# Turning the second 128 prompt queries' probabilities on VectorE instead of TensorE

## The chip, the cores and the metric

One Trainium2 chip, one NeuronCore. The metric is the device time of one execution in microseconds; lower is better. The time before is the median of three runs, 1886.21 us (1886.2 to 1886.69).

## The reference: one layer of a hybrid streaming encoder

There are 320 tokens: 64 of a sample (with 128 cached positions) and 256 of a prompt. All of them go through one layer:

```
u = rmsnorm(h) @ w_in            # q, k, v of mixer A (chunk band) and of mixer B (forgetting), forget logits, two gates
scores = q @ k^T * scale + bias  # 8 heads x 128 in each mixer; bias is a table (A) or F[t] - F[s] (B), masked
probs  = softmax(scores)
o      = probs @ v
h += (sigmoid(gate_A) * (o_A @ w_a) + sigmoid(gate_B) * (o_B @ w_b)) @ w_o
h += relu(rmsnorm(h) @ w_up)^2 @ w_down
h += (p @ w_ple_proj) * sigmoid(rmsnorm(h) @ w_ple_gate)
y  = rmsnorm(h)
```

In the attention of one head and mixer the prompt has two groups of 128 queries. The first group sees 128 keys, so its probabilities are a 128x128 block. The second group sees 256 keys, so it has two such blocks. The sample's 64 queries see 192 keys.

## The kernel before

**Layout.** Activations are kept transposed: 128 features in the partitions, 320 tokens in the columns. Every weight matrix is cut into slabs of 128 output columns and 1024 input rows. Two slabs make a panel, which is one 128x320 product. A slab is loaded by SP (512 KB, four slots), rounded by ScalarE to its high part (`split_weights`, L628), and VectorE takes the low part as the rest (`split_weights`, L945). TensorE multiplies a slab in 24 matmuls (L395 to L397: high by high, high by low, low by high). TensorE waits for a slab at `s_wlo`, which VectorE counts up after L945. ScalarE waits at `s_mul` until TensorE is through with the slab that last filled the slot, and SP waits at `s_wlo` until the raw slab in it was read.

**Units.** There are 16 attention units: 8 heads by 2 mixers, written (head, mixer). While TensorE multiplies the three panels (q, k, v) of one unit, the attention of the unit before runs in the gaps. TensorE's order in `unit` (L446) is: panel t; `attend` of the unit two back; `scores` of the unit before; panel t+1; the first half of panel t+2; `turn` of the unit before; the second half of panel t+2. Unit (0,0) to (1,0) are handled by straight-line code, then a loop over the heads 2 to 7 holds two units in its body. The last units end beside the first panels of the merge stage (L510 to L512): after the first half of the first merge panel come `attend` of (7,0) and `scores` of (7,1), in the middle of the second merge panel comes `turn` of (7,1), and after that panel `attend` of (7,1).

**The path of the probabilities.** VectorE adds the bias and finds the maxima (`logits`, L984 to L990), ScalarE takes the exponentials (L688), VectorE the reciprocal of their sums (`invert`, L996), and GpSimd multiplies by it (`normalise`, L1346), in the order first prompt group, second prompt group, sample, each counting `s_prob` up. To multiply with the values, the probabilities must stand with the keys in the partitions. For the prompt, TensorE turns three 128x128 blocks against an identity (`turn`, L424 to L426) into the bank TURNED, and ScalarE copies 384 columns to `probs_t` (`copy_turned`, L695). For the sample, VectorE turns them in squares of 32x32, two squares in an instruction, eight instructions (`turn_sample`, L1028). VectorE turns the values in the same manner, 16 instructions of three squares (`turn_values`, L1017). `attend` (L428) waits for the copy, for the sample's turn (`s_sturned`) and for the values.

**VectorE's order.** It is written out by hand in its own `unit` (L1138): take q out of its bank; low part of slab (t+2, half 0); `split_output`, the low part of the attention output (L1002); `logits`; slab (t+2, half 1); `invert`; `turn_values`; take k out; slab (t+3, half 0); `turn_sample`; slab (t+3, half 1); take v out; both slabs of panel t+4. Unit (0,0) has its own straight line (L1130 to L1136): take k out, split panel 6, take v out, `turn_values`, `turn_sample`, split panel 7. The last unit too has its own (L1185 to L1200).

Of the kernel before, what the change touches and what calls it, by code (L numbers as in the profile page):

```python
# [21 lines left out]
ACT = mybir.ActivationFunctionType  # L22
AX_X = mybir.AxisListType.X

P = 128
# [24 lines left out]
P0, P1, P2 = S1, S1 + P, S1 + P + SEQ  # L50
# [4 lines left out]
T_MERGE = T_UNIT + 3 * UNITS  # L55
# [65 lines left out]
def hybrid_layer(nc, io):  # L121
    from contextlib import ExitStack

    with ExitStack() as ctx:
        def sb(name, shape, dt=F32):
            return ctx.enter_context(nc.sbuf_tensor(name, shape, dt))

        def sem(name):
            return ctx.enter_context(nc.semaphore(name))
# [26 lines left out]
        ident = sb("ident", [P, P])  # L156
# [21 lines left out]
        probs = sb("probs", [P, P2])  # L178
        probs_t = sb("probs_t", [P, 512])
# [3 lines left out]
        banks = ctx.enter_context(nc.psum_tensor("banks", [P, 8, 512], F32))  # L183
        SCORES, SAMPLE, VALUES, TURNED = 4, 5, 6, 7
# [21 lines left out]
        def f32(ap):  # L206
            return ap.bitcast(F32)
# [62 lines left out]
        s_prob = sem("probs_ready")  # L270
        s_vrows = sem("value_rows_ready")
        s_sturned = sem("sample_probs_turned")
        s_turn = sem("prompt_probs_turned")
        s_tcopy = sem("turned_prompt_probs_ready")
        s_pv = sem("attended")
# [34 lines left out]
        def after(eng, s, value):  # L310
            if not isinstance(value, int) or value > 0:
                eng.wait_ge(s, value)
# [55 lines left out]
        def _(pe):  # L368
            def multiply(t, hi, lo, ready=None, value=None, bank_read=False, second=None, between=None, base=0):

                pe_bank = base + t.half
                if bank_read:

                    pe.wait_ge(s_acc, t.first - 1)
                for half in range(2):
                    if half and between:  # L380
                        between()

                    pe.wait_ge(s_wlo, t.count(2, half + 1))
                    slot = 2 * t.half + half
                    for kk in range(SLAB_KB):
                        k = half * SLAB_KB + kk
                        if k == KB - 1 and ready:

                            pe.wait_ge(ready, value)
                        bank = pe_bank if second is None or half == 0 else second  # L390
                        out = banks[:, bank, 0:TOK]
                        ws = slice(kk * P, (kk + 1) * P)
                        xs = slice(k * TOK, (k + 1) * TOK)
                        lo_k, hi_k = (0, KB - 1) if second is None else (half * SLAB_KB, half * SLAB_KB + SLAB_KB - 1)
                        nc.tensor.matmul(out, w_hi[:, slot, ws], hi[:, xs], start=k == lo_k, stop=False)  # L395
                        nc.tensor.matmul(out, w_hi[:, slot, ws], lo[:, xs], start=False, stop=False)  # L396
                        mm = nc.tensor.matmul(out, w_lo[:, slot, ws], hi[:, xs], start=False, stop=k == hi_k)  # L397
                    mm.then_inc(s_mul, 1)
# [16 lines left out]
                nc.tensor.matmul(banks[:, SCORES, P:P + SEQ], q[:, NEW + P:TOK], k[:, S1:KEYS], start=True, stop=True)  # L415
                nc.tensor.matmul(banks[:, SAMPLE, S0:S1], q[:, 0:P], k[:, 0:S1], start=True, stop=True).then_inc(s_score, 1)  # L416

            def turn(u):

                pe.wait_ge(s_prob, u.count(3, 2))  # L420

                after(pe, s_tcopy, u.count())
                b = banks[:, TURNED, 0:3 * P]
                nc.tensor.transpose(b[:, 0:P], probs[:, P0:P1], ident[:, :])  # L424
                nc.tensor.transpose(b[:, P:2 * P], probs[:, P1:P1 + P], ident[:, :])
                nc.tensor.transpose(b[:, 2 * P:3 * P], probs[:, P1 + P:P2], ident[:, :]).then_inc(s_turn, 1)  # L426

            def attend(u):  # L428

# [13 lines left out]
            def mix_in(t, between=None, bank_read=False):  # L443
                multiply(t, x_hi, x_lo, between=between, bank_read=bank_read)
# [55 lines left out]
            with pe.Fori(2, HEADS) as i:  # L500
                t = Panel(T_UNIT, 6, i)
                unit(t, Unit(i - 1, 0), Unit(i - 1, 1))
                unit(t.plus(3), Unit(i - 1, 1), Unit(i, 0))
            last = Unit(HEADS - 1, 1)
# [3 lines left out]
                scores(last)  # L508

            mix_in(Panel(T_MERGE), between=last_scores)  # L510
            mix_in(Panel(T_MERGE + 1), between=lambda: turn(last))
            attend(last)  # L512
            merge(Panel(T_MERGE + 2), first=True)
            mix_in(Panel(T_MERGE + 3))
# [2 lines left out]
            with pe.Fori(1, KB // 2) as i:  # L517
                t = Panel(T_MERGE, 6, i)
# [34 lines left out]
            for s in range(4):  # L553
# [6 lines left out]
                for n in range(4):  # L560
                    out = banks[:, 4 * (1 - s % 2) + n, 0:TOK]
                    for k in range(2):
                        b = 2 * n + k
# [57 lines left out]
        def _(act):  # L621
            def split_weights(t, halves=(0, 1)):
                for half in halves:
                    slot = 2 * t.half + half

                    act.wait_ge(s_slab[slot], t.loads())
                    after(act, s_mul, t.count(2, half - SLOTS + 1))
                    nc.scalar.activation(w_hi[:, slot, :], w_raw[:, slot, :], ACT.Copy).then_inc(s_whi, 1)  # L628
# [59 lines left out]
                    nc.scalar.activation(probs[0:rows, a:b], probs[0:rows, a:b], ACT.Exp, bias=neg_max[0:rows, c:c + 1],  # L688
                                         accum_out=exp_sum[0:rows, c:c + 1]).then_inc(s_exp, 1)

            def copy_turned(u):

                act.wait_ge(s_turn, u.count(1, 1))
                after(act, s_pv, u.count())
                nc.scalar.activation(probs_t[:, P:4 * P], banks[:, TURNED, 0:3 * P], ACT.Copy).then_inc(s_tcopy, 1)  # L695

            def split_output(u):

# [94 lines left out]
            with act.Fori(2, HEADS) as i:  # L793
                t = Panel(T_UNIT, 6, i)
# [21 lines left out]
            last = Unit(HEADS - 1, 1)  # L816
            t = Panel(T_MERGE)
# [4 lines left out]
            split_weights(t.plus(2), (1,))  # L822
            sigmoid(t, 0, 1)
            split_weights(t.plus(3), (0,))
            copy_turned(last)
            split_weights(t.plus(3), (1,))
            sigmoid(t.plus(1), 2, 3)
            split_output(last)
# [8 lines left out]
            with act.Fori(1, KB // 2) as i:  # L837
                t = Panel(T_MERGE, 6, i)
# [9 lines left out]
            with act.Fori(0, KB // 2) as i:  # L848
                for j in range(2):
                    t = Panel(T_OUT + j, 2, i)  # L850
# [38 lines left out]
            with act.Fori(0, KB // 2) as i:  # L889
                for j in range(2):  # L890
                    t = Panel(tq + KB + j, 2, i)
# [47 lines left out]
        def _(dve):  # L939
            def split_weights(t, halves=(0, 1)):  # L940
                for half in halves:
                    slot = 2 * t.half + half

                    dve.wait_ge(s_whi, t.count(2, half + 1))
                    nc.vector.tensor_tensor(w_lo[:, slot, :], w_raw[:, slot, :], f32(w_hi[:, slot, :]), ALU.subtract).then_inc(s_wlo, 1)  # L945
# [58 lines left out]
            def by_block(t, first, count, stride, at):  # L1004

                return t[:, first:first + count * stride].rearrange("p (n c) -> p n c", n=count)[:, :, at:at + 32]

            def turn_values(u, rows=range(4)):

                if 0 in rows:  # L1010

                    after(dve, s_pv, u.count())
                    dve.wait_ge(s_acc, u.count(3, T_UNIT + 3))
                for i in rows:
                    for j in range(4):
                        src = by_block(v_t[u.mixer][32 * i:32 * i + 32], 0, 3, P, 32 * j)
                        tr = nc.vector.transpose(by_block(v_rows[32 * j:32 * j + 32], 0, 3, P, 32 * i), src)  # L1017
                if 3 in rows:
                    tr.then_inc(s_vrows, 1)

            def turn_sample(u):

                dve.wait_ge(s_prob, u.count(3, 3))
                after(dve, s_pv, u.count())
                for i in range(NEW // 32):
                    for j in range(4):
                        src = by_block(probs[32 * i:32 * i + 32, 32 * j:32 * j + P], 0, 2, NEW, 0)
                        tr = nc.vector.transpose(by_block(probs_t[32 * j:32 * j + 32], 0, 2, NEW, 32 * i), src)  # L1028
                tr.then_inc(s_sturned, 1)
# [102 lines left out]
            evacuate(Panel(T_UNIT + 5), Unit(0, 1), 2)  # L1132
            dve.wait_ge(s_zero, 4)
            turn_values(Unit(0, 0))
            turn_sample(Unit(0, 0))
            split_weights(Panel(7))  # L1136

            def unit(t, earlier, before, this):  # L1138
                evacuate(t, this, 0)
                split_weights(t.plus(2), (0,))  # L1140
                split_output(earlier)
                logits(before)
                split_weights(t.plus(2), (1,))
                invert(before)
                turn_values(before)
                evacuate(t.plus(1), this, 1)
                split_weights(t.plus(3), (0,))
                turn_sample(before)
                split_weights(t.plus(3), (1,))
                evacuate(t.plus(2), this, 2)  # L1150
                split_weights(t.plus(4))

# [2 lines left out]
            with dve.Fori(2, HEADS) as i:  # L1155
                t = Panel(T_UNIT, 6, i)
# [28 lines left out]
            last = Unit(HEADS - 1, 1)  # L1185
            t = Panel(T_MERGE)
# [14 lines left out]
            with dve.Fori(1, KB // 2) as i:  # L1201
                t = Panel(T_MERGE, 6, i)
# [8 lines left out]
            with dve.Fori(0, KB // 2) as i:  # L1211
                for j in range(2):
                    t = Panel(T_OUT + j, 2, i)
# [21 lines left out]
            with dve.Fori(1, KB // 2) as i:  # L1235
                for j in range(2):
                    t = Panel(T_FF + j, 2, i)
                    hidden(t, i * 2 + j, i * 2 + j)
                    split_weights(t.plus(2))
            with dve.Fori(0, KB // 2) as i:  # L1240
                for j in range(2):
                    t = Panel(T_FF + KB + j, 2, i)
                    add_to_h(t, i * 2 + j)
                    split_weights(t.plus(2))
            with dve.Fori(1, QUARTERS - 1) as quarter:
                with dve.Fori(0, KB // 2) as i:
                    for j in range(2):
                        t = Panel(T_FF + j, 2, quarter * KB + i)
                        hidden(t, quarter * KB + i * 2 + j, i * 2 + j)
                        split_weights(t.plus(2))  # L1250
                with dve.Fori(0, KB // 2) as i:
                    for j in range(2):
                        t = Panel(T_FF + KB + j, 2, quarter * KB + i)
# [3 lines left out]
            with dve.Fori(0, KB // 2) as i:  # L1257
                for j in range(2):
                    t = Panel(tq + j, 2, i)
                    hidden(t, i * 2 + (QUARTERS - 1) * KB + j, i * 2 + j)  # L1260
                    split_weights(t.plus(2))
            with dve.Fori(0, KB // 2) as i:
                for j in range(2):
                    t = Panel(tq + KB + j, 2, i)
# [212 lines left out]
```

## Time and profile before

| what | value |
| --- | --- |
| median of three runs | 1886.21 us |
| the profiled execution | 1886.27 us |
| its span in the trace | 1884.5 us |
| TensorE busy | 1874.9 us, 99% |
| VectorE busy | 987.0 us, 52% |
| ScalarE busy | 710.9 us, 38% |
| GpSimd busy | 178.8 us, 9% |
| mean granted TensorE clock | 0.999 |

The 1.8 us between the profiled execution and its span lie before the first and after the last instruction. The shares are averages over stages: from 100 to 200 us, in the attention units, VectorE is busy 70.64 us of 100; from 600 to 1200 us, in the channel mixer, 282.75 us of 600. Matmul records overlap, since one starts before the one ahead has ended; so the pace of TensorE is read from the distance between starts, not from the durations.

### The profile page before, as it was taken

What the parts mean: (1) busy time and instruction counts of PE and PEld (TensorE: products, weight loads), DVE (VectorE), ACT (ScalarE), POOL (GpSimd) and SP (SyncE); (2) the same over time, 40 slices, a digit from 0 to 9 for tenths busy, and PEclk for the clock granted to TensorE, in tenths of its full rate; (3) what the DMA queues carried; (4) which work ended last, traced back from release to release, by engine and by line L of the source; (5) the groups of instructions that cost most, each with busy time, mean ns of one, the idle gap of its engine ahead of it and who ended that gap; (6) DMA issues with size and microseconds to landing.
All of it is one profiled execution on the core that took longest, in us unless ns stands there. A gap on an engine that the chain in (4) does not pass through costs nothing.

```text
span 1884.5 us, 35125 instructions
## 1 busy us (share of the span) xinstructions
PE 1874.9 (99%) x12803; PEld 1871.0 (99%) x12803; DVE 987.0 (52%) x1505; ACT 710.9 (38%) x885; POOL 178.8 (9%) x280
## 2 busy tenths in 40 slices
PE   9999999999999999999999999999999999999998
PEld 9999999999999999999999999999999999999998
DVE  8766666674444445555444344434443444555544
ACT  6333333343333333333333333333332333333564
POOL 0111111110000001221100001000100000122121
PEclk9999999999999999999999999999999999999999
DMA  7554554545444444444444444444444444444442
GB/s 264 177 168 166 163 166 165 164 147 200 155 136 157 153 154 135 155 148 150 156 156 145 145 147 143 156 156 138 152 155 154 145 148 145 144 156 147 154 146 100
DMA packets 94310, 292.42 MB, mean 155 GB/s; under 512 B 13072, under 2 KB 26536, under 8 KB 94120
## 3 DMA queue, kind: packets, MB, share of 16 engines
q1 hardware_dynamic: 75760, 275.32, 44.2%
q10 hardware_dynamic: 18520, 16.69, 3.0%
q8 instruction: 20, 0.33, 0.1%
q14 instruction: 10, 0.08, 0.0%
HBM read 284.08 MB, written 9.46 MB: 156 GB/s over the span
## 4 chain that ended last, share of the span: by engine, by line
PE 99%; DVE 0%; DMA 0%; ACT 0%; issue 0%; SPq 0%; ACTq 0%
PE banks L395 32%; PE banks L397 31%; PE banks L396 31%; PE banks L463 0%; PE banks L464 0%; PE banks L465 0%; PE banks L415 0%; PE banks L416 0%; PE banks L567 0%; PE banks L566 0%; PE banks L568 0%; DMA h<-in_x_t 0%; PE banks L439 0%; PE banks L438 0%; PE banks L441 0%; PE banks L440 0%
## 5 line engine op out<-in xcount | busy, mean ns | idle before, releaser
L628 ACT ACTIVATE w_hi<-w_raw 128x1024 fp32r<-128x1024 f32 x510 | 538.7, 1059 | 985.9 <-PE banks L397 978.8
L395 PE MATMUL banks<-x_hi,w_hi 128*128 128x320 f32 x2512 | 780.2, 311 | 0.0
L397 PE MATMUL banks<-x_hi,w_lo 128*128 128x320 f32 x2512 | 776.2, 309 | 0.0
L396 PE MATMUL banks<-x_lo,w_hi 128*128 128x320 f32 x2512 | 776.1, 309 | 0.0
L945 DVE TENSOR_TENSOR w_lo<-w_raw,w_hi 128x1024 fp32r<-128x1024 f32 x510 | 602.5, 1217 | 20.9 <-ACT w_hi L628 20.4
L396 PEld LDWEIGHTS banks<-x_lo,w_hi 128*128 128x128 f32 x2512 | 471.7, 188 | 0.2
L395 PEld LDWEIGHTS banks<-x_hi,w_hi 128*128 128x128 f32 x2512 | 471.6, 188 | 0.2
L397 PEld LDWEIGHTS banks<-x_hi,w_lo 128*128 128x128 f32 x2512 | 471.5, 188 | 0.0
L395 PE MATMUL banks<-o_hi,w_hi 128*128 128x320 f32 x1280 | 395.6, 309 | 0.0
L396 PE MATMUL banks<-o_lo,w_hi 128*128 128x320 f32 x1280 | 395.5, 309 | 0.0
L397 PE MATMUL banks<-o_hi,w_lo 128*128 128x320 f32 x1280 | 395.5, 309 | 0.0
L395 PEld LDWEIGHTS banks<-o_hi,w_hi 128*128 128x128 f32 x1280 | 240.3, 188 | 0.0
L396 PEld LDWEIGHTS banks<-o_lo,w_hi 128*128 128x128 f32 x1280 | 240.3, 188 | 0.0
L397 PEld LDWEIGHTS banks<-o_hi,w_lo 128*128 128x128 f32 x1280 | 240.3, 188 | 0.0
L1207 DVE TENSOR_TENSOR h<-banks,h 128x320 f32 x80 | 39.5, 493 | 263.3 <-PE banks L397 263.3
L1381 POOL TENSOR_TENSOR tmp<-tmp 128x320 f32<-128x320 f32 x64 | 46.1, 721 | 741.6 <-DVE tmp L1221 741.6
L1221 DVE SCALAR_TENSOR_TENSOR tmp<-banks,rstd 128x320 f32<-128x320 f32 x64 | 31.5, 491 | 137.6 <-PE banks L397 137.6
L1370 POOL TENSOR_TENSOR sq<-h 128x320 f32 x47 | 33.9, 720 | 586.3 <-DVE h L1207 505.8
L1161 DVE TENSOR_TENSOR tmp<-banks,rstd 128x320 f32<-128x320 f32 x47 | 23.1, 492 | 122.2 <-PE banks L397 122.2
L1225 DVE TENSOR_TENSOR o_lo<-tmp,o_hi 128x320 f32 (+1 forms) x64 | 31.5, 493 | 104.6 <-ACT o_hi L858 103.3
L395 PE MATMUL banks<-m_hi,w_hi 128*128 128x320 f32 x256 | 79.1, 309 | 0.0
L396 PE MATMUL banks<-m_lo,w_hi 128*128 128x320 f32 x256 | 79.1, 309 | 0.0
(154 smaller groups left out, 1084.7 us busy)
## 6 DMA issues: line engine op xcount, KB each, us to landing
w_raw<-in_w_slabs SPq DMA_DIRECT2D x515, 512.0 KB, 4.0
out_kv_t<-k_t ACTq DMA_DIRECT2D x16, 160.0 KB, 2.7
out_kv_t<-v_t ACTq DMA_DIRECT2D x16, 160.0 KB, 2.8
h<-in_x_t ACTq DMA_DIRECT2D x1, 2560.0 KB, 10.2
out_y<-y_rows SPq DMA_DIRECT2D x4, 512.0 KB, 4.0
h<-in_x_t SPq DMA_DIRECT2D x3, 640.0 KB, 9.6
f_keys<-f_rows ACTq DMA_DIRECT2D x8, 224.0 KB, 4.0
bias_rows<-in_rel_rows ACTq DMA_DIRECT2D x1, 1024.0 KB
```

The source lines that it names most:

```text
L395: nc.tensor.matmul(out, w_hi[:, slot, ws], hi[:, xs], start=k == lo_k, stop=False)
L396: nc.tensor.matmul(out, w_hi[:, slot, ws], lo[:, xs], start=False, stop=False)
L397: mm = nc.tensor.matmul(out, w_lo[:, slot, ws], hi[:, xs], start=False, stop=k == hi_k)
L628: nc.scalar.activation(w_hi[:, slot, :], w_raw[:, slot, :], ACT.Copy).then_inc(s_whi, 1)
L945: nc.vector.tensor_tensor(w_lo[:, slot, :], w_raw[:, slot, :], f32(w_hi[:, slot, :]), ALU.subtract).then_inc(s_wlo, 1)
L1161: nc.vector.tensor_tensor(tm(dst), summed(t, base), rstd[:, :], ALU.mult).then_inc(s_acc, 1)
L1207: nc.vector.tensor_tensor(blk(h, n), summed(t), blk(h, n), ALU.add).then_inc(s_acc, 1)
L1221: nc.vector.scalar_tensor_tensor(out=tm(0), in0=acc, scalar=0.0, in1=rstd[:, :], op0=ALU.max, op1=ALU.mult).then_inc(s_acc, 1)
L1225: nc.vector.tensor_tensor(blk(o_lo, n), tm(1), f32(blk(o_hi, n)), ALU.subtract).then_inc(s_olo, 1)
L1370: nc.gpsimd.tensor_tensor(sq[:, :], blk(h, n), blk(h, n), ALU.mult).then_inc(s_sq, 1)
L1381: nc.gpsimd.tensor_tensor(tm(1), tm(0), tm(0), ALU.mult).then_inc(s_sqr, 1)
```

## The change

`turn` on TensorE turns only the first block, and all three in the last unit. `copy_turned` copies 128 columns instead of 384, and 384 in the last unit. A new `turn_second` on VectorE turns the second group's two blocks: it waits for the second of the three normalisations and for `attend` of the unit before (as `turn_sample` does), and has 16 instructions of two 32x32 squares. It counts up no semaphore of its own: `turn_sample`, behind it in VectorE's order, does. In `unit` it stands where `turn_sample` stood, and `turn_sample` moves behind the low part of slab (t+3, half 1). In the straight line of unit (0,0) it stands between `turn_values` and `turn_sample`.

```diff
-            def turn(u):
+            def turn(u, is_last=False):
 
-                pe.wait_ge(s_prob, u.count(3, 2))
+                pe.wait_ge(s_prob, u.count(3, 2 if is_last else 1))
 
                 after(pe, s_tcopy, u.count())
                 b = banks[:, TURNED, 0:3 * P]
-                nc.tensor.transpose(b[:, 0:P], probs[:, P0:P1], ident[:, :])
-                nc.tensor.transpose(b[:, P:2 * P], probs[:, P1:P1 + P], ident[:, :])
-                nc.tensor.transpose(b[:, 2 * P:3 * P], probs[:, P1 + P:P2], ident[:, :]).then_inc(s_turn, 1)
+                tr = nc.tensor.transpose(b[:, 0:P], probs[:, P0:P1], ident[:, :])
+                if is_last:
+                    nc.tensor.transpose(b[:, P:2 * P], probs[:, P1:P1 + P], ident[:, :])
+                    tr = nc.tensor.transpose(b[:, 2 * P:3 * P], probs[:, P1 + P:P2], ident[:, :])
+                tr.then_inc(s_turn, 1)
...
-                nc.scalar.activation(probs_t[:, P:4 * P], banks[:, TURNED, 0:3 * P], ACT.Copy).then_inc(s_tcopy, 1)
+                cols = 3 * P if is_last else P
+                nc.scalar.activation(probs_t[:, P:P + cols], banks[:, TURNED, 0:cols], ACT.Copy).then_inc(s_tcopy, 1)
...
+            def turn_second(u):
+
+                dve.wait_ge(s_prob, u.count(3, 2))
+                after(dve, s_pv, u.count())
+                for i in range(4):
+                    for j in range(4):
+                        src = by_block(probs[32 * i:32 * i + 32], P1, 2, P, 32 * j)
+                        nc.vector.transpose(by_block(probs_t[32 * j:32 * j + 32], 2 * P, 2, P, 32 * i), src)
...
             turn_values(Unit(0, 0))
+            turn_second(Unit(0, 0))
             turn_sample(Unit(0, 0))
             split_weights(Panel(7))
...
                 split_weights(t.plus(3), (0,))
+                turn_second(before)
+                split_weights(t.plus(3), (1,))
                 turn_sample(before)
-                split_weights(t.plus(3), (1,))
                 evacuate(t.plus(2), this, 2)
```

## Rows read from the trace of the kernel before

**Rows 1.** The page: busy time of each engine, us (share of the span) xinstructions.
```profile
PE 1874.9 (99%) x12803; PEld 1871.0 (99%) x12803; DVE 987.0 (52%) x1505; ACT 710.9 (38%) x885; POOL 178.8 (9%) x280
```

**Rows 2.** Timeline, TensorE at a turn: start us, us, engine line, operation [idle before].
```profile
311.98 0.31 PE L397 MATMUL banks<-x_hi,w_lo 128*128 128x320 f32 x1
312.13 0.27 PE L424 MATMUL banks<-ident,probs 128*128 128x128 f32 x1
312.24 0.27 PE L425 MATMUL banks<-ident,probs 128*128 128x128 f32 x1
...
312.61 0.30 PE L396 MATMUL banks<-x_lo,w_hi 128*128 128x320 f32 x1
312.75 0.31 PE L397 MATMUL banks<-x_hi,w_lo 128*128 128x320 f32 x1
```

**Rows 3.** Timeline, VectorE around the turns of unit (0,0).
```profile
57.00 0.49 DVE L975 TENSOR_TENSOR v_t<-banks,rstd 128x320 f32<-128x320 f32 x1 [2.29 <-PE banks L397]
57.41 4.51 DVE L1017 STREAM_TRANSPOSE v_rows<-v_t 32x96 f32<-32x96 f32 x16
61.95 1.98 DVE L1028 STREAM_TRANSPOSE probs_t<-probs 32x64 f32<-32x64 f32 x8
63.96 2.43 DVE L945 TENSOR_TENSOR w_lo<-w_raw,w_hi 128x1024 fp32r<-128x1024 f32 x2
```

**Rows 4.** Timeline, TensorE at the attend of unit (0,0).
```profile
63.69 0.31 PE L397 MATMUL banks<-x_hi,w_lo 128*128 128x320 f32 x1
64.03 0.41 PE L437 MATMUL banks<-probs_t,v_cache 128*128 128x64 f32 x2
```

**Rows 5.** Timeline, VectorE in the unit that turns (0,1).
```profile
78.79 1.97 DVE L1028 STREAM_TRANSPOSE probs_t<-probs 32x64 f32<-32x64 f32 x8
80.79 1.23 DVE L945 TENSOR_TENSOR w_lo<-w_raw,w_hi 128x1024 fp32r<-128x1024 f32 x1
```

**Rows 6.** Timeline, TensorE: first matmul of the slab split at 80.79.
```profile
84.12 0.31 PE L395 MATMUL banks<-x_hi,w_hi 128*128 128x320 f32 x1
```

**Rows 7.** Timeline, VectorE in the loop, the unit that turns (6,0).
```profile
323.21 0.49 DVE L970 SCALAR_TENSOR_TENSOR q_t<-banks,rstd 128x320 f32<-128x320 f32 x1 [3.90 <-PE banks L397]
...
328.18 0.49 DVE L1002 TENSOR_TENSOR o_lo<-banks,o_hi 128x320 f32 x1 [3.34 <-ACT o_hi L700]
...
337.37 1.98 DVE L1028 STREAM_TRANSPOSE probs_t<-probs 32x64 f32<-32x64 f32 x8
339.37 1.23 DVE L945 TENSOR_TENSOR w_lo<-w_raw,w_hi 128x1024 fp32r<-128x1024 f32 x1
```

**Rows 8.** Timeline, TensorE: first matmul of the slab split at 339.37.
```profile
343.04 0.31 PE L395 MATMUL banks<-x_hi,w_hi 128*128 128x320 f32 x1
```

**Rows 9.** Timeline, GpSimd: the three normalisations in that unit.
```profile
331.65 2.24 POOL L1346 TENSOR_SCALAR probs<-probs,inv_sum 128x128 f32<-128x128 f32 x3 [21.57 <-DVE inv_sum L996]
```

**Rows 10.** Timeline, VectorE from the turns of (7,0) to those of (7,1).
```profile
384.45 1.97 DVE L1028 STREAM_TRANSPOSE probs_t<-probs 32x64 f32<-32x64 f32 x8
...
387.99 2.35 DVE L945 TENSOR_TENSOR w_lo<-w_raw,w_hi 128x1024 fp32r<-128x1024 f32 x2
392.00 0.49 DVE L1002 TENSOR_TENSOR o_lo<-banks,o_hi 128x320 fp32r<-128x320 f32 x1 [1.65 <-ACT o_hi L700]
...
401.34 1.97 DVE L1028 STREAM_TRANSPOSE probs_t<-probs 32x64 f32<-32x64 f32 x8
```

**Rows 11.** Timeline, TensorE: the first matmuls of the attends of (7,0) and (7,1).
```profile
390.11 0.33 PE L437 MATMUL banks<-probs_t,v_cache 128*128 128x64 f32 x2
...
403.42 0.29 PE L437 MATMUL banks<-probs_t,v_cache 128*128 128x64 f32 x1 [0.17 <-issue]
```

**Rows 12.** Busy time by stretch (PE, PEld, DVE, ACT, POOL; then granted clock, DMA share, GB/s).
```profile
1878.00:1880.00 2.00, 0.16 (x2) 0.00 (x0) 0.84 (x2) 0.45 (x1) 0.00 (x0) 1.00 1.01 231
1880.00:1882.00 2.00, 0.00 (x0) 0.00 (x0) 0.00 (x0) 0.00 (x0) 0.00 (x0) 0.55 1.02 410
```

**Rows 13.** Timeline, TensorE: the 17 matmuls on zeros at the start.
```profile
1.46 5.95 PE L477 MATMUL banks<-m_lo 128*128 128x512 f32 x17 [1.46 <-DVE m_lo L1036]
```

More of the change, by code:

```diff
@@ L510, in _ @@
             mix_in(Panel(T_MERGE), between=last_scores)
-            mix_in(Panel(T_MERGE + 1), between=lambda: turn(last))
+            mix_in(Panel(T_MERGE + 1), between=lambda: turn(last, True))
             attend(last)
@@ L689, in exps, with copy_turned @@
                                          accum_out=exp_sum[0:rows, c:c + 1]).then_inc(s_exp, 1)
-            def copy_turned(u):
+            def copy_turned(u, is_last=False):
                 act.wait_ge(s_turn, u.count(1, 1))
                 after(act, s_pv, u.count())
-                nc.scalar.activation(probs_t[:, P:4 * P], banks[:, TURNED, 0:3 * P], ACT.Copy).then_inc(s_tcopy, 1)
+                cols = 3 * P if is_last else P
+                nc.scalar.activation(probs_t[:, P:P + cols], banks[:, TURNED, 0:cols], ACT.Copy).then_inc(s_tcopy, 1)
             def split_output(u):
@@ L824, in _ @@
             split_weights(t.plus(3), (0,))
-            copy_turned(last)
+            copy_turned(last, True)
             split_weights(t.plus(3), (1,))
```

## The prediction

> **What bounds the kernel now.** The page first: TensorE is busy 99% of the span, the others half of it or less [rows 1]. So an edit counts for what it takes from TensorE's row of starts, or for the time it makes TensorE wait. VectorE's mean share (52%) says nothing on the latter: what matters is when it has a slab or a turn ready against the moment TensorE needs it. So I read the timelines of both engines side by side in four places: a turn in the loop, the straight line of unit (0,0), the loop's ordinary unit, and the loop's end.
>
> **What TensorE saves.** Two of three turns go in each of 15 units. The starts at L424 and L425 are 0.11 us apart, though each lasts 0.27 us [rows 2]. From the last L397 before the turn to the second matmul after it are 0.63 us, where without a turn 2 x 0.147 = 0.29 would do (312.61 to 312.75 is one such step), so the three cost 0.34 together [rows 2], and two of them 2 x 0.11 = 0.22 us. Bounds: 0.20 (the third's own entry cost stays) and 0.34 (all goes). In sum at most 15 x 0.22 = 3.3 us, if TensorE never waits.
>
> The Trainium skill (TensorE: Matmul & The Clock Gate, Part 4: PE-mode transpose) puts such a turn at about 275 ns in one kernel's context. The trace has that duration (0.27), but a pace of 0.11; two turns by the page would save 0.55 us a unit, which is a rival below.
>
> **What VectorE pays.** `turn_second` has 16 instructions of the form of `turn_sample` (32x64). Eight of those take 61.95 to 63.96 = 2.01 us [rows 3], so 16 take 4.02. From below, 16 x 0.235 = 3.8 would be their durations laid end to end; from above 16 of the 32x96 form take 4.54 (57.41 to 61.95) [rows 3]. I take 4.02. Its wait for GpSimd costs nothing: in the loop the normalisations are over at 333.9 and it starts at 337.4 [rows 7, 9]. ScalarE's copy gets shorter, which nobody waits for.
>
> **Unit (0,0).** VectorE takes v out at 57.00 as soon as TensorE gives it (idle 2.29 before it), turns the values until 61.95 and the sample until 63.93 [rows 3]. TensorE's attend starts at 64.03, 0.34 after the last L397 where 0.15 would be its pace, so it already waits for that turn, some 0.1 us behind its end [rows 4]. Now 4.02 us stand in between with no cover. The first term, 57.00, comes 0.22 earlier. The attend is late by 4.02 - 0.22 = **+3.8 us**, and everything behind it with it: TensorE has nothing else to do, as attend is next in its order.
>
> **Unit (0,1).** Between slab (t+3, half 0) and slab (t+3, half 1) there now stand 4.02 instead of 2.01 us. That slab was split at 80.79 + 1.23 = 82.02 [rows 5] and was needed at 84.12 [rows 6]: 2.10 of room. 2.10 - 2.01 - 0.22 (TensorE is there earlier) - 0.10 (from VectorE's end to TensorE's start, as above) = -0.2: TensorE waits what the turn saved. **0.0 us.**
>
> **Units (1,0) to (6,1), 12 of them.** The same slab: split at 340.60 [rows 7], needed at 343.04 [rows 8], 2.44 of room in units of mixer A (2.7 to 2.9 in those of mixer B). 2.44 - 2.01 - 0.22 - 0.10 = 0.1 is left: hidden, but only just. The rest of the 4.02 falls into VectorE's idle 3.90 before taking q out, of which 0 is left, and then into the 3.34 before `split_output` [rows 7], so the next unit's softmax starts no later. `turn_sample`, now behind that slab, runs from 342.5 to 344.5; the attend behind it is due one slab after 343.04, 24 x 0.147 = 3.5 us, so at 346.3. Slab loads are asked for up to 4 us later, but ScalarE waits for TensorE to free the slot anyway. So **12 x -0.22 = -2.6 us**; if the 0.1 is really -0.1, six of them lose half of it, +0.6.
>
> **The loop's end.** The last turn of the loop is that of (7,0), and here only one half panel stands between the slab and the attend, not two. VectorE: `turn_second` 384.45 to 388.47 [rows 10], slab to 389.6, `turn_sample` to 391.6; attend 391.7 instead of 390.11 [rows 11], +1.6. What follows costs more still: before, VectorE was idle 1.65 before `split_output` at 392.00 and is then busy without a gap until `turn_sample` of (7,1) ends at 403.31, and the attend of (7,1) starts 0.11 behind it, at 403.42 [rows 10, 11]. VectorE sets that attend. The two slabs of 387.99 now end at 390.34 + 4.02 = 394.4, and `split_output` starts right behind, at 394.3: **+2.3 us** at the attend of (7,1), which contains the 1.6; the turn of (7,0) saves nothing here. From then on TensorE is the bound again to the end, nothing gives it back.
>
> **The clock.** In unit (0,0) TensorE will stand idle some 4.0 us (63.8 to 67.8). The only stretch of the trace with such a pause is the end: TensorE is busy only 0.16 us from 1878 to 1880, so until about 1878.2, and the grant is 1.00 there and 0.55 from 1880 to 1882, so it fell from 2.4 to 1.2 GHz at about 1880.2, 2 us into the pause [rows 12]. So a fall is likely in the stall. Its price no row shows. At the start 17 matmuls take 5.95 us [rows 13], which at the pace of the 320-column ones (0.147) would take 13 x 0.235 + 4 x 0.117 = 3.5 us: a low clock costs at most 2.4 us until it is back. Below it is 0. I take **+1.3 us**, about the middle, as part of the low time will pass in the idle itself.
>
> **Sum.** 3.8 + 0 - 2.6 + 2.3 = +3.5 without the clock, +4.8 with it. The profiled execution took 1886.27 (span 1884.5), so the span is to be 1889.3 and the time 1891.1; the median stood 0.06 lower, so 1891.0 us, +0.25%.
>
> **Rivals.**
> The clock holds through the stall. Then 1889.8 us. For it: the mean grant over the span is 0.999, and the pause is the only one of its kind. Against: [rows 12].
>
> VectorE becomes the bound of the loop: the 0.1 us of room is used up by jitter, by the turns running at 0.28 us as the wide form does [rows 3], or by contention with GpSimd. The price is 16 x 0.03 = 0.5 us more for the turns, of which 0.4 shows in six loop units and nothing in the other six, and 0.5 at (0,0), (0,1) and the loop's end: 2.4 + 1.5 = +3.9, 1895.0 us with the clock.
>
> A turn costs TensorE its duration. Then two are worth 0.54 us: 4.02 - 0.54 = 3.5 at (0,0), nothing at (0,1), six loop units save 0.34 (all the room they have) and six 0.54, so -5.3, and +2.3: +0.5, 1886.7 us. It decides from 0.47 a unit on. Against it: starts of 0.11 apart [rows 2]. It is not slower only if the clock holds too.
>
> VectorE's turns are cheaper in a long row: at a pace p for 16 the sum is 2 x 16p - 1.7 - 0.2 - 2.8 (the wait at (0,1) gone), which is below zero from p = 0.15 us down; at 0.11, -1.2, 1885.1 us or, were both stalls fully covered, 15 x -0.22 = 1883.0. Against it: eight already stand in a row and show 0.25, sixteen wide ones 0.28 [rows 3].
>
> That the change does not move the work, I give nothing: instructions are in the diff one by one.
>
> **Chances.** Stalls plus fallen clock 0.62 (1890.3 to 1892.8); stalls, clock holds 0.17 (1889.8); VectorE bounds the loop 0.10; dear turns on TensorE 0.06; cheap ones on VectorE 0.05. A measurement here tells 0.2%, 3.8 us, from no change: slower is beyond 1890.0, faster below 1882.4. The first and third case are slower (0.72, of which I give 0.04 to a cheap fall of the clock), the second is just within, the fourth within; of the fifth 0.04 would be beyond. Faster 0.04, same 0.28, slower 0.68. The range reaches from 1888.2, a turn worth 0.34 with a clock that holds (3.5 - 1.6), to 1893.8, the full price of the clock (3.5 + 2.4, 1892.2) and some 1.6 of the 3.9 of a bound VectorE.
>
> **What would show it.** L425 and L426 once, not 16 times; VectorE 16 transposes of 32x64 more in 15 units. TensorE's waits get a new first row: L437 behind `turn_sample`, about 3.9 us at 68 us, and two smaller ones near 393 and 407. Attends in between stand 23.3 apart instead of 23.54 (first gap 23.6). In a table of stretches all of the difference lies before 410 us, +3.5 to 5, and the granted clock dips near 68 us. I am wrong if the gaps stay at 23.54 (no saving, or VectorE bounds), or if the attend of (0,0) does not move by 3.8.

## The result and the profile after

The changed kernel takes 1894.27 us (median of 5 runs, 1893.8 to 1896.94) against 1886.2 for the kernel before (5 runs): +8.1 us, ratio 1.0045, interval 1.0034 to 1.0056. The forecast was 1891.0 us in a range of 1888.2 to 1893.8. So the direction was right, the size was too small, and the time lies outside the range.

Line numbers of this kernel are a few higher: the turns on VectorE are L1031 (`turn_second`) and L1040 (`turn_sample`), the low part of a slab is L948, `attend` starts at L439. The page and its chain:

```profile
PE 1877.7 (99%) x12773; PEld 1872.0 (99%) x12773; DVE 1042.3 (55%) x1745; ACT 707.0 (37%) x885; POOL 179.3 (9%) x280
PE 96%; DVE 2%; issue 1%; ACTq 1%; DMA 0%; ACT 0%; DVEq 0%; SPq 0%
```

VectorE has 55 us more of work (240 turns), and the chain now runs 2% over VectorE and 1% over ScalarE's queue. TensorE's waits, longest in total first (us in total, times, longest):

```profile
PE banks L439 <- issue: 6.3, 3, 4.0
...
PE banks L395 <- DVE w_lo L948: 0.8, 3, 0.3
```

The first row is new but for 0.2 us: three attends that wait. The last is new altogether: slabs that are late. It shows only part of what they cost, since idle time counts from the end of the matmul record ahead, which overlaps the next start. Where the time went, by the starts of the attends in both profiled executions (before 1884.5 us of span, after 1894.1; this execution of after took 1895.95, 1.7 above its median):

| stretch | before | after | difference | forecast |
| --- | --- | --- | --- | --- |
| attend of (0,0) | 64.03 | 67.70 | +3.7 | +3.8 |
| to attend of (0,1) | 23.61 | 26.38 | +2.8 | 0.0, clock +1.3 |
| 12 units, to attend of (6,1) | 282.45 | 281.97 | -0.5 | -2.6 |
| to attend of (7,0) | 20.02 | 22.10 | +2.1 | +1.6 |
| to attend of (7,1) | 13.31 | 15.02 | +1.7 | +0.7 |
| sum | | | +9.8 | +4.8 |

Of the 12 units in the third row seven are 23.32 or 23.33 us long, as forecast, and five are 23.53 to 23.92: 2.1 us of late slabs in all.

**A turn.** TensorE of the changed kernel at the turn of (0,1), to be laid beside [rows 2] (start us, us):

```profile
106.59 0.31 PE L397 MATMUL banks<-x_hi,w_lo 128*128 128x320 f32 x1
106.74 0.27 PE L424 MATMUL banks<-ident,probs 128*128 128x128 f32 x1
...
106.99 0.31 PE L396 MATMUL banks<-x_lo,w_hi 128*128 128x320 f32 x1
```

From the last L397 to the second matmul behind the turn are 0.40 us instead of 0.63. The quiet units (those in which TensorE waits for nothing) are 23.32 us long instead of 23.54: the turns save 0.22 each, as forecast, though a turn's record is 0.27 long.

**The first attend.** VectorE after, answering to [rows 3], and TensorE, answering to [rows 4]:

```profile
57.10 4.51 DVE L1020 STREAM_TRANSPOSE v_rows<-v_t 32x96 f32<-32x96 f32 x16
61.64 3.98 DVE L1031 STREAM_TRANSPOSE probs_t<-probs 32x64 f32<-32x64 f32 x16
65.63 1.97 DVE L1040 STREAM_TRANSPOSE probs_t<-probs 32x64 f32<-32x64 f32 x8
```
```profile
63.38 0.31 PE L397 MATMUL banks<-x_hi,w_lo 128*128 128x320 f32 x1
67.70 0.66 PE L439 MATMUL banks<-probs_t,v_cache 128*128 128x64 f32 x2 [4.01 <-issue]
```

The sixteen take 3.99 from start to start, and the attend starts 0.1 behind the end of the sample's turn. Its own record is 0.66 long instead of 0.41: the clock. Stretches of the changed kernel (columns as in [rows 12]):

```profile
64.00:66.00 2.00, 0.00 (x0) 0.00 (x0) 1.89 (x9) 0.84 (x1) 0.00 (x0) 1.00 0.00 0
66.00:68.00 2.00, 0.30 (x2) 0.33 (x2) 1.89 (x8) 0.00 (x0) 0.00 (x0) 0.80 0.00 0
...
72.00:74.00 2.00, 2.00 (x9) 2.00 (x8) 0.82 (x2) 0.44 (x1) 0.00 (x0) 0.50 1.01 301
74.00:76.00 2.00, 2.00 (x15) 2.00 (x15) 2.00 (x6) 1.32 (x2) 0.00 (x0) 0.99 0.86 264
```

0.80 in 66 to 68 means 0.8 us at half, so the grant fell to 1.2 GHz at 67.2, near the pause's end, and came back at 74.0. It was low for 6.8 us, of which only 0.5 lay in the idle.

**A late slab in the loop.** VectorE and TensorE in the unit that turns (1,1), from 131 us on; the L948 at 136.29 splits the slab of the L395 at 137.57:

```profile
132.31 3.97 DVE L1031 STREAM_TRANSPOSE probs_t<-probs 32x64 f32<-32x64 f32 x16
136.29 1.23 DVE L948 TENSOR_TENSOR w_lo<-w_raw,w_hi 128x1024 fp32r<-128x1024 f32 x1
137.43 1.97 DVE L1040 STREAM_TRANSPOSE probs_t<-probs 32x64 f32<-32x64 f32 x8
```
```profile
137.05 0.31 PE L397 MATMUL banks<-x_hi,w_lo 128*128 128x320 f32 x1
137.57 0.42 PE L395 MATMUL banks<-x_hi,w_hi 128*128 128x320 f32 x1 [0.21 <-DVE w_lo L948]
```

The two starts are 0.52 apart where 0.15 is the pace. The turns took what they should; the whole row of VectorE started late in this unit. ScalarE shows why (ACTq is its queue of DMAs, us is how long the issue took). In this unit the third of the five issues ahead of L703 took 1.36 us:

```profile
119.89 1.36 ACTq L662 DMA_DIRECT2D bias<-bias_rows  x1
...
122.53 0.44 ACT L703 ACTIVATE o_hi<-banks 128x320 f32 x1 [3.87 <-issue]
```

In the unit after it, one of mixer B, it was the issue of k_t:

```profile
144.56 1.02 ACTq L673 DMA_DIRECT2D k_t<-in_k_cache_t  x1
...
146.42 0.44 ACT L703 ACTIVATE o_hi<-banks 128x320 f32 x1 [3.97 <-issue]
```

L703 stands behind five DMA issues in ScalarE's order, and VectorE's `split_output`, with everything behind it, waits for it. In the kernel before, the issue of k_t took 0.47 in each of the loop's six units of mixer B, and no issue in the loop took over 0.6.

The length of a unit follows the start of L703 closely. In the five traces with this order on ScalarE and the second group turned on VectorE (the changed kernel and e1, e2, e6, e7 below), take the 11 units from the attend of (1,0) to that of (6,1). In all 55 the distance between attends is 23.32 us plus what L703 starts later than 4.63 us behind the attend, within 0.02 us: nothing is added up to 4.61, and 0.47 at 5.12, 0.60 at 5.22, 1.35 at 5.98.

**The loop's end.** The changed kernel, answering to [rows 10] and [rows 11]:

```profile
390.95 3.97 DVE L1031 STREAM_TRANSPOSE probs_t<-probs 32x64 f32<-32x64 f32 x16
394.94 1.23 DVE L948 TENSOR_TENSOR w_lo<-w_raw,w_hi 128x1024 fp32r<-128x1024 f32 x1
396.08 1.97 DVE L1040 STREAM_TRANSPOSE probs_t<-probs 32x64 f32<-32x64 f32 x8
...
401.10 0.49 DVE L1005 TENSOR_TENSOR o_lo<-banks,o_hi 128x320 fp32r<-128x320 f32 x1 [0.26 <-ACT o_hi L703]
402.17 0.56 DVE L987 TENSOR_TENSOR probs<-banks,bias 128x384 f32<-128x384 f32 x1 [0.58 <-PE banks L416]
```
```profile
398.15 0.54 PE L439 MATMUL banks<-probs_t,v_cache 128*128 128x64 f32 x2 [2.14 <-issue]
...
413.17 0.41 PE L439 MATMUL banks<-probs_t,v_cache 128*128 128x64 f32 x2 [0.16 <-issue]
```

The wait is there, with slab and sample's turn behind `turn_second`. Its issue of k_t took 1.01, so VectorE was 0.5 us later than reckoned, and the clock fell a second time (0.57 from 398 to 400), so that VectorE now waited for slow scores (0.58 at 402.17).

### The profile page after: what moved, and what is told of

Read it like the earlier page. It is cut to its first block, busy times and chain, and to the rows that moved or that the text cites. A ratio compares the mean times of both kernels' runs of the same rounds, so it can differ in the third digit from the quotient of the medians.

```text
span 1894.1 us, 35331 instructions
## 1 busy us (share of the span) xinstructions
PE 1877.7 (99%) x12773; PEld 1872.0 (99%) x12773; DVE 1042.3 (55%) x1745; ACT 707.0 (37%) x885; POOL 179.3 (9%) x280
## 4 chain that ended last, share of the span: by engine, by line
PE 96%; DVE 2%; issue 1%; ACTq 1%; DMA 0%; ACT 0%; DVEq 0%; SPq 0%
PE banks L395 30%; PE banks L397 30%; PE banks L396 30%; DVE v_rows L1020 1%; DVE w_lo L948 1%; DVE probs_t L1031 1%; PE banks L465 0%; PE banks L467 0%; PE banks L466 0%; PE banks L415 0%; PE banks L441 0%; PE banks L570 0%; PE banks L568 0%; PE banks L569 0%; PE banks L416 0%
## 5 line engine op out<-in xcount | busy, mean ns | idle before, releaser
L395 PE MATMUL banks<-x_hi,w_hi 128*128 128x320 f32 x2512 | 781.3, 311 | 0.8 <-DVE w_lo L948 0.8
L397 PE MATMUL banks<-x_hi,w_lo 128*128 128x320 f32 x2512 | 776.5, 309 | 0.0
L948 DVE TENSOR_TENSOR w_lo<-w_raw,w_hi 128x1024 fp32r<-128x1024 f32 x510 | 602.4, 1217 | 20.5 <-ACT w_hi L630 20.2
L395 PEld LDWEIGHTS banks<-x_hi,w_hi 128*128 128x128 f32 x2512 | 472.0, 188 | 2.4 <-DVE w_lo L948 2.1
L397 PEld LDWEIGHTS banks<-x_hi,w_lo 128*128 128x128 f32 x2512 | 471.9, 188 | 0.0
L395 PE MATMUL banks<-o_hi,w_hi 128*128 128x320 f32 x1280 | 395.6, 309 | 0.0
L397 PE MATMUL banks<-o_hi,w_lo 128*128 128x320 f32 x1280 | 395.5, 309 | 0.0
L395 PEld LDWEIGHTS banks<-o_hi,w_hi 128*128 128x128 f32 x1280 | 240.2, 188 | 0.0
L397 PEld LDWEIGHTS banks<-o_hi,w_lo 128*128 128x128 f32 x1280 | 240.2, 188 | 0.0
L395 PE MATMUL banks<-m_hi,w_hi 128*128 128x320 f32 x256 | 79.1, 309 | 0.0
```

## The experiments

Theory A: TensorE waits at the two ends of the unit stage behind `turn_second`; the first wait lets the clock fall; and in the loop the later split of two slabs makes SP ask for slabs at the time when ScalarE issues its DMAs. Some of these issues then last longer and hold VectorE up. Its rivals are named with each run. Times are medians of 6 to 10 runs, beside 25 of the kernel before, but for the last. The changed kernel was not run again beside them, so a difference to its 1894.27 has the spread between occasions in it: the kernel before had medians of 1886.20, 1886.47 and 1886.34. The ratios are to the kernel before. One execution of each kernel was traced. The forecasts of e1, e6 and e7 take terms off the median 1894.3 that were read from the traced execution, which took 1895.95; so they came out up to 1.7 us too low, and there the traced executions are compared too.

**e1_first**

```diff
-            unit(Panel(T_UNIT + 3), None, Unit(0, 0))
+            unit(Panel(T_UNIT + 3), None, Unit(0, 0), True)
...
-            copy_turned(Unit(0, 0))
+            copy_turned(Unit(0, 0), True)
...
-            turn_second(Unit(0, 0))
```

> The changed kernel, but unit (0,0) is turned as before: three turns on TensorE, no turn_second on VectorE. Theory A (the wait of TensorE at the attend of (0,0), 3.7 us, and the clock that falls in it, 3.0 us): both go, 1894.3 - 6.7 = 1887.6 us, granted clock 1.00 near 68 us. Rival B (the loss sits in the loop, the first unit only shifts it): under 2 us less, 1892.5 or more. The wait at the attend of (7,0) stays in both, with its fall of the clock.

1889.35 us, ratio 1.0015 (1.0006 to 1.0025), 4.9 less than the changed kernel. The first attend is at 64.13 and the clock holds through the whole stage. Rival B is out. The median is 1.7 above theory A's time, but the traced executions are 1895.95 - 1889.2 = 6.75 us apart, against 6.7 forecast. Of these, 3.6 are the wait at (0,0), 2.7 the clock behind it, 0.1 the loop (281.90 against 281.97) and 0.35 the end. There the fall of the clock that was expected did not come (14.01 to the last attend instead of 15.02), while the wait before (7,0) was longer (22.76 instead of 22.10). The loop's waits are shared out otherwise: one slab is 1.1 us late,

```profile
341.31 0.31 PE L397 MATMUL banks<-x_hi,w_lo 128*128 128x320 f32 x1
342.72 0.41 PE L395 MATMUL banks<-x_hi,w_hi 128*128 128x320 f32 x1 [1.10 <-DVE w_lo L948]
```

and 17.7 us ahead of that start ScalarE's issue of k_t took four times its usual 0.47:

```profile
325.01 1.93 ACTq L673 DMA_DIRECT2D k_t<-in_k_cache_t  x1
```

**e2_both_ends**

```diff
-            with pe.Fori(2, HEADS) as i:
+            with pe.Fori(2, HEADS - 1) as i:
...
+            unit(end, Unit(HEADS - 2, 0), Unit(HEADS - 2, 1))
+            unit(end.plus(3), Unit(HEADS - 2, 1), Unit(HEADS - 1, 0), True)
# the same on ScalarE and VectorE, on top of e1_first
```

> As e1_first, and unit (7,0) too is turned by TensorE (the last pass of the head loop is written out for it). Theory A: the +3.8 us of the two last attends go as well, what is left is the 13 units between: 13 x -0.22 = -2.8 us of turns and +2.1 us of waits of TensorE for slab (t+3, half 1), so 1885.5 us. Rival B (the waits in the loop are noise of one execution): 1883.4. Rival C (the end costs nothing by itself): 1887.6 as e1_first.

1886.49 us, ratio 0.9998 (0.9989 to 1.0008): 2.9 less than e1_first. The gaps to the last two attends are 20.02 and 13.31 again, so rival C is out, and B too: the 12 loop units take 282.71 us against 282.45 before. They save 2.6 in turns and lose 2.9 in waits. With both ends undone, the change in the loop alone is worth nothing. The time is 1.0 above theory A's, which had 2.1 for the waits. They follow the issues unit by unit (attends are counted from 0, that of (0,0)):

| unit (gap between attends from its start) | issue of k_t, us | gap, us |
| --- | --- | --- |
| attend 3 | 1.45 | 24.25 |
| attend 5 | 1.05 | 23.85 |
| attend 7 | 1.07 | 23.87 |
| attend 9 | 1.14 | 23.91 |
| attend 11 | 0.52 | 23.46 |
| attends 4, 6, 8, 10 | 0.34 | 23.31 to 23.32 |

**e6_warm**

```diff
                 mix_in(t)
+                if warm:
+                    pe.wait_ge(s_tcopy, 1)
+                    for _ in range(warm):
+                        nc.tensor.matmul(banks[:, TURNED, 0:TOK], blk(m_lo, 8, 2)[:, 0:P], blk(m_lo, 8, 2)[:, 0:TOK], start=True, stop=True)
...
-            unit(Panel(T_UNIT + 6), Unit(0, 0), Unit(0, 1))
+            unit(Panel(T_UNIT + 6), Unit(0, 0), Unit(0, 1), warm=24)
```

> The changed kernel, and TensorE does 24 matmuls on zeros (128x320, 3.5 us) in the wait ahead of the attend of (0,0). Theory A (of the 6.4 us at the first two attends 3.0 are the fallen clock): the attend of (0,0) still starts at 67.7, the granted clock stays 1.00 there, the time is 1891.3. Rival B (the slow attend, scores and panel behind the wait have another cause, such as VectorE's lateness): clock up, but the time stays within 0.7 us of 1894.3.

1892.62 us, ratio 1.0033 (1.0021 to 1.0046). The attend starts at 67.68, the same place, and the clock stays:

```profile
66.00:68.00 2.00, 1.49 (x11) 1.26 (x11) 1.89 (x8) 0.00 (x0) 0.00 (x0) 1.00 0.00 0
68.00:70.00 2.00, 2.00 (x17) 1.95 (x17) 2.00 (x3) 0.00 (x0) 0.00 (x0) 1.00 0.07 6
```

The stretch to the next attend is 23.65 instead of 26.38, so the fall cost 2.7 us in the traced execution. Rival B is out. The median is 1.3 above the forecast. The traced executions are 3.5 us apart (1892.45 against 1895.95), of which 2.7 are the first fall and 1.0 the second one, at the loop's end, which did not come here either. Between the medians it is 1.7 in all. What the fall costs varies: in e3_reorder below the same pause brought a low stretch of 3.4 us instead of 6.8, and a cost of 1.6 us (25.03 to the next attend against 23.39 in e4_first_reorder, where the fall is absent).

**e7_early**

```diff
+            turn_second(Unit(0, 0))
+            turn_sample(Unit(0, 0))
             evacuate(Panel(T_UNIT + 5), Unit(0, 1), 2)
             dve.wait_ge(s_zero, 4)
             turn_values(Unit(0, 0))
-            turn_second(Unit(0, 0))
-            turn_sample(Unit(0, 0))
```

> The changed kernel, but in unit (0,0) VectorE turns the second group and the sample before it takes v out and turns the values, so that 2.3 us of its idle time lie under them. Theory A (the wait is VectorE's row of work behind 57.0 us and nothing else): the attend of (0,0) starts near 65.6 instead of 67.7, a pause of 1.9 us; the clock falls for one window less or not at all: 1894.3 - 2.1 - 3.0 = 1889.2, with a partial fall 1890.7. Rival B (the pause length does not matter to the clock): 1892.2.

1891.08 us, ratio 1.0026 (1.0015 to 1.0037), 3.2 less than the changed kernel. The attend is at 65.69, as forecast, so the first wait is indeed VectorE's row of work behind 57 us. The clock held through its pause (idle 1.90 us): 23.64 to the next attend. The median lies between the 1889.2 of theory A (1890.7 with a partial fall) and the 1892.2 of rival B, so it does not decide between them. The traced executions are 5.9 us apart (1890.04 against 1895.95), where theory A has 5.1: 2.0 at (0,0), 2.7 of clock behind it, 1.6 at the loop's end, less 0.4 for longer slab waits in the loop (attends 24.33, 24.18 and 23.97 apart). In this one traced execution the shorter pause went without a fall, which agrees with theory A and is against rival B; it is no proof that the length decides (see the last section).

**e3_reorder**

```diff
-                load_unit(this)
                 split_output(earlier)
-                store_kv(before)
                 exps(before)
+                load_unit(this)
+                store_kv(before)
```

> The changed kernel, and in ScalarE's unit order the five DMAs of load_unit (and store_kv) are issued behind split_output and exps instead of ahead of them, so that VectorE's split_output, and all of its row behind it, no longer wait for them. Theory A (the loop loses its gain because the slab loads, now asked for later, make some of ScalarE's DMA issues last 1 to 2 us, and o_lo with them): o_lo starts about 1.9 us behind the attend instead of 4.7 to 5.8, no wait for slab (t+3, half 1), the gaps between attends are 23.32 in all loop units, and the wait at (7,0) goes, as VectorE is some 2.5 us earlier; left are 3.7 us at (0,0) and 3.0 of clock: 1886.3 + 6.7 - 3.1 = 1889.9 us. Rival B (the slab waits come from VectorE's own load, whatever the order of ScalarE's DMAs): gaps of 23.8 stay, 1893 us or more.

1888.89 us, ratio 1.0016 (1.0006 to 1.0026), 5.4 less than the changed kernel. All 12 gaps of the loop are 23.32 or 23.33 and the one to (7,0) is 19.80; no wait for a slab is left in TensorE's list. VectorE does the same work as in the changed kernel, so it was not its load by itself: rival B is out. What is left is the wait at (0,0) and its clock, which cost 1.6 us here instead of the 3.0 taken; so the time is 1.0 under the forecast. ScalarE here, in the unit at 140 us: `split_output` comes first, and the issues stand behind the exponentials, where nobody waits for them.

```profile
141.27 0.44 ACT L703 ACTIVATE o_hi<-banks 128x320 f32 x1 [0.24 <-PE banks L443]
...
145.97 0.49 ACTq L673 DMA_DIRECT2D k_t<-in_k_cache_t  x1
```

`o_hi` starts 1.5 us behind the attend in every loop unit, so nothing in the issues can delay it. The issues of k_t in the loop's units of mixer B are 0.47 to 0.51 too. Why they are short again this run does not separate, because two things moved. The issue comes 6.2 us behind the attend instead of 3.4. And SP asks for slabs up to 3 us earlier than in the changed kernel, since VectorE is no longer held up:

| kernel | SP's last three requests ahead of the issue of k_t (us from the attend; units of mixer B behind a quiet unit) | issue of k_t at |
| --- | --- | --- |
| before | -4.6, -3.5, 2.0 | 3.4 |
| changed | -0.5, 0.7, 2.2 | 3.4 |
| e3_reorder | -2.0, 2.0, 5.4 | 6.2 |
| e8_late_loads (below) | -0.7, 0.5, 2.0 | 3.4 |

**e4_first_reorder** (the edits of e1_first and e3_reorder together)

> e1_first (unit (0,0) turned by TensorE) and e3_reorder together. Theory A: no wait at (0,0), none in the loop, none at (7,0): 14 x -0.22 = -3.1 us and the 0.3 that the attend of (7,1) waited before, 1886.3 - 3.4 = 1882.9 us, faster than both kernels. Rival B: at least the wait at the end stays, since the sample's turn is still behind turn_second: 1885.

1883.39 us (10 runs, 1882.9 to 1883.7), ratio to the kernel before 0.9984 (0.9975 to 0.9994): faster than both kernels, by 3.0 and 10.9 us. Its gaps are 23.39, 12 x 23.32, 19.80, 13.31, that is 14 x -0.22 = -3.1 us. The 0.3 us at the last attend, which I also expected to go, stayed:

```profile
399.79 0.31 PE L397 MATMUL banks<-x_hi,w_lo 128*128 128x320 f32 x1
400.27 0.41 PE L439 MATMUL banks<-probs_t,v_cache 128*128 128x64 f32 x2 [0.18 <-issue]
```

The last unit's code is its own, and there `split_output` is ahead of the DMA issues in both kernels. VectorE takes `o_lo` at 388.83, 1.9 us behind the attend of (7,0), and is then busy until its turn of the sample ends at 400.17, so it still sets this attend: 13.31 us behind the one ahead, as before. In the loop VectorE has room again; before taking q out it is idle

```profile
344.13 0.49 DVE L973 SCALAR_TENSOR_TENSOR q_t<-banks,rstd 128x320 f32<-128x320 f32 x1 [2.43 <-PE banks L397]
```

where in [rows 7] it was 3.90 with 4 us less of work.

**e5_before_reorder** (the edit of e3_reorder on the kernel before)

> The kernel before with the same new order of ScalarE's DMAs alone. Theory A (in the kernel before nothing waits for VectorE but the attend of (7,1)): 1886.0, within 0.4 us of before; the three turns stay on TensorE, gaps 23.54. Rival B (the order by itself brings what e4_first_reorder brings): 1883.

1886.29 us, ratio 1.0001 (0.9991 to 1.0010): nothing. The gaps are 23.53 or 23.54, so rival B is out. Here the order of the DMAs is worth something only once VectorE's row is short of room.

**e8_late_loads** (the kernel before, with 16 turns of 32x64 into `tmp`, whose result nobody reads)

```diff
                 split_weights(t.plus(3), (1,))
+                idle_turns(before)
                 evacuate(t.plus(2), this, 2)
```

> The kernel before, all turns as before, but in each unit from (0,1) on VectorE does 16 transposes of 32x64 into unused cells between slab (t+3, half 1) and taking v out, so that the two slabs of panel t+4 are split 4 us later and SP asks for the next slabs as late as in the changed kernel. Theory A (the time at which slabs are asked for lengthens ScalarE's DMA issues): in the loop's units of mixer B the issue of k_t at L671 is no longer 0.47 each time but up to 1 to 1.5 in several of them, and o_lo starts later by as much; the attends stay 23.54 apart, as the room of 2.4 us covers it; the time moves by under 1 us. Rival B (the lengthened issues come from another thing that the change brings): all issues as in the kernel before.

One run, 1889.06 us. The issues did lengthen: in the loop's units of mixer B k_t took 0.88, 0.94, 1.39, 0.47, 0.47 and 0.75. One of them, and its effect on VectorE:

```profile
232.19 1.39 ACTq L672 DMA_DIRECT2D k_t<-in_k_cache_t  x1
```
```profile
234.90 0.49 DVE L1003 TENSOR_TENSOR o_lo<-banks,o_hi 128x320 f32 x1 [4.24 <-ACT o_hi L701]
```

`split_output` was 0.9 us later than in the kernel before, and the attends stayed 23.54 apart in all loop units, as the 2.4 us of room cover it. In every loop unit of mixer B traced in the kernel before and in e5_before_reorder that issue took 0.47 or 0.48. So late splits alone, with all turns of probabilities as before, are enough to lengthen the issues: rival B is out, with the reserve that this is one execution. The time was a miss, +2.7 instead of under 1, and not by the issues: at the loop's end the 16 turns stand ahead of taking v out, which comes at 391.86, so the scores of (7,1) wait for it (L415, 1.1 us), and the attend of (7,1) comes 2.5 us late.

## Why the prediction was right or wrong

**The turns on TensorE, right.** 0.22 us a unit: e3_reorder and e4_first_reorder have it in each unit. The rival of a full duration each is out; that was 0.27 us by the trace and about 275 ns by the Trainium skill (TensorE: Matmul & The Clock Gate, Part 4: PE-mode transpose). The trace has the page's duration, but two turns are worth 0.22 us and not 0.55. The rival's "It decides from 0.47 a unit on" does not follow from its own terms: they give a sum of +1.0 at 0.47 and of zero only at 0.61. Nothing hangs on it.

**The cost of `turn_second`, right.** 4.02 forecast, 3.99 measured.

**Unit (0,0), right.** +3.8 forecast, +3.7 measured, gone in e1_first. For unit (0,1) 0.0 was forecast; where the clock holds it is 23.64 (e6_warm, e7_early) against 23.61.

**The clock: the fall was forecast rightly, its price was too small, and a second fall was left out.** The step said: "a low clock costs at most 2.4 us until it is back", and took 1.3, "as part of the low time will pass in the idle itself". It cost 2.7 us in the profiled execution. The bound was made from the 17 matmuls at the start, which took 2.4 us more than at full pace; here the grant stayed at 1.2 GHz for 6.8 us, and it fell only near the end of the pause, so that just 0.5 of it passed in the idle. A second fall at the loop's end was not in the forecast at all, though its own wait of 1.6 us stood in the sum; e1_first, whose clock holds, has 14.01 us there against 15.02, so it cost 1.0. In the traced execution the clock is thus 3.7 us where 1.3 was taken.

**The 12 loop units, wrong, and this is the step that failed.** "2.44 - 2.01 - 0.22 - 0.10 = 0.1 is left: hidden, but only just", and "Slab loads are asked for up to 4 us later, but ScalarE waits for TensorE to free the slot anyway." The arithmetic of the room was right: the quiet units are 23.32 us long. But the room of 2.44 was read off units in which ScalarE's issues ran undisturbed, and the change moves SP's requests to just ahead of these issues. What that does to ScalarE's queue was put at nothing. The row of VectorE hangs on `o_hi`, which stands behind the issues; each start of it later than 4.63 us behind the attend went into the unit's length. Measured: -0.5 instead of -2.6 (e2_both_ends: +0.3). The rival "VectorE becomes the bound of the loop" had the right place with the wrong reason, as slow turns and GpSimd have no part in it. Its forecast of 1895.0 was near the time by luck: 1.5 us of its sum lay at places that cost nothing of the kind.

**The loop's end, right in kind.** +2.3 forecast, +3.8 measured: 0.5 by a lengthened issue, 1.0 by the clock. In e7_early, which has neither (k_t 0.47, clock 1.00), it is 21.57 and 14.00, that is +1.6 and +0.7, both as forecast. In e2_both_ends all is gone, though an issue of f_query took 2.40 us there.

In sum: of the 5.0 us between forecast and the profiled execution, 2.1 are slab waits in the loop, some 1.4 the first fall of the clock, 1.0 the second, 0.5 the issue at the end. So lengthened issues and the clock have about equal parts in the miss (2.6 and 2.4). The median is 1.7 lower. No trace shows which of these terms is smaller there. The mean grant (0.997 against 0.996) would fit a shorter fall, but the clock cannot be all of the spread: the longest of the five executions (1896.94) has the highest grant, 0.998. The slab waits vary too, from 2.1 to 2.9 us in the five traces.

## What to carry to other kernels

When an edit delays an engine's row, follow also the queue that waits for that engine: its requests move too, and what they meet then is not in the trace of before. A margin of 0.1 us, read from a trace in which a neighbour ran undisturbed, is no margin. Here the work that may be late (the DMA issues of the next unit) stood ahead of the work that may not (`split_output`); two lines in the other order gave the edit its whole gain in the loop, though in the kernel before they are worth nothing. The rest of the -3.1 us needed unit (0,0) left to TensorE: with the order alone the kernel was still slower than before, 1888.89 us.

## What was not expected of the hardware

An issue of a 64 KB DMA from ScalarE's queue (k_t, units of mixer B) takes 0.47 us in every loop unit of the kernel before, and up to 1.93 us in the loop where SP's requests for 512 KB slabs come 1.2 and 2.7 us ahead of it. It is not only this load: bias took 1.36 once (changed kernel) and f_query 2.40 (e2_both_ends). Why it is 0.47 in one unit and 1.4 in the next alike one is open: SP's requests come at the same moments in both. The number of slabs under way and the small f_query loads ahead of k_t (1.0 and 0.2 KB) were not separated.

The length of a pause alone does not say whether the clock falls. TensorE was idle ahead of the attend of (7,0) for 2.14 us in the changed kernel and in e6_warm; the grant fell from 2.4 to 1.2 GHz at 398.3 in the first and held in the second. It held through 1.90 us (e7_early) and through 2.79 us (e1_first) as well. In the pause of 4.0 us at (0,0), or 1.0 us behind its end, it fell both times that it was traced, once for 6.8 us and once for 3.4 us. What decides between the cases was not tried.
